# A hybrid decoder step on 8 cores: another order of work in the first two input projections

## The reference, cut to what matters

```python
h = _rmsnorm(x, norm_mix)
proj = h @ w_in                       # (B,T,2048) -> u | gb | gc | v, 512 channels each
d = trailing means of u over 2/4/8/16 positions, minus u   # 4 groups of 128 channels
a = einsum('btgc,gcd->btgd', d, w_pool) * pool_scale
conv = dwconv3_causal(gc * v)         # 3 taps
b = gb * conv
x = x + concat(a, b) @ w_out
h = _rmsnorm(x, norm_ffn)
up = dwconv3_causal(h @ w_up) + bias  # 5632 channels
x = x + (silu(gate) * val) @ w_down
y = _rmsnorm(x, norm_final)
```

## Time and profile before

| | |
|---|---|
| median of 3 runs | 730.68 us (727.58 to 747.07) |
| the profiled execution: time | 728.0 us |
| its span on the slowest core, core 3 | 726.4 us |
| spans of cores 0, 2, 4, 6 | 720.5, 720.9, 720.6, 720.1 us |
| spans of cores 1, 3, 5, 7 | 725.9, 726.4, 724.7, 724.5 us |
| PE busy | 689.3 us, 95% |
| stage 3 of tile 0 begins on core 3 at | 125.5 us |

### The profile page before, as it was taken

How to read it: one execution, slowest core, us unless ns; L and a number is a source line. 1 busy time by engine, 2 the same in 40 slices (tenths; PEclk the granted TensorE clock), 3 DMA queues, 4 the chain that set the end, 5 groups by cost and what they waited for, 6 DMA issues and landing times.

```text
span 726.4 us, 12730 instructions; the slowest of 8 cores (720.1 to 726.4 us)
## 1 busy us (share of the span) xinstructions
PE 689.3 (95%) x3788; PEld 334.7 (46%) x3788; DVE 492.2 (68%) x846; ACT 347.0 (48%) x809; POOL 215.5 (30%) x414
## 2 busy tenths in 40 slices
PE   5869799889999999999999999999999999999996
PEld 4534345445554454444444444444444444444442
DVE  4277767578886245788878566877777276888724
ACT  4344342567775112877643233766621234666521
POOL 2242100467774000455431000444420001443300
PEclk8989899989999999999999999999999999999999
DMA  8998593887787456999989430999987212980002
GB/s 198 234 170 125 97 214 62 131 146 132 126 137 152 67 164 166 172 189 187 184 150 164 145 117 1 177 166 163 155 144 123 105 71 54 162 135 1 4 29 88
DMA packets 26742, 94.62 MB, mean 130 GB/s; under 512 B 3358, under 2 KB 3742, under 8 KB 26674
## 3 DMA queue, kind: packets, MB, share of 16 engines
q0 software_dynamic: 18288, 66.59, 56.5%
q1 hardware_dynamic: 8242, 26.95, 11.1%
q10 hardware_dynamic: 144, 0.26, 0.1%
HBM read 150.36 MB, written 10.01 MB: 221 GB/s over the span
## 4 chain that ended last, share of the span: by engine, by line
PE 82%; DMA 7%; DVE 5%; issue 2%; ACT 2%; DVEq 0%; SPq 0%; ACTq 0%; POOL 0%; POOLq 0%
PE G L598 53%; PE G L905 12%; PE G L906 12%; DMA wslot<-w_str 3%; DMA yp<-x1b 3%; PE TR L598 2%; PE TR L554 2%; PE G L1142 1%; DMA x1b<-xp 1%; DVE w_down_sb L769 1%; DVE arena L769 1%; ACT hbuf L496 0%; DVE arena L830 0%; DVE arena L842 0%; DVE actT L558 0%
## 5 line engine op out<-in xcount | busy, mean ns | idle before, releaser
L969 ACT ACTIVATE arena<-G,cst_sb 128x512 f32<-128x512 f32 x176 | 135.4, 776 | 86.2 <-PE G L598 85.1
L598 PE MATMUL G<-aT,wslot 128*128 128x512 bf16 x736 | 165.8, 383 | 1.3 <-DVE arena L1007 1.0
L998 DVE SCALAR_TENSOR_TENSOR arena<-G,cst_sb,arena 128x512 f32<-128x512 f32 x176 | 124.0, 747 | 43.7 <-ACT Esave L974 41.0
L598 PE MATMUL G<-aT,sm_arena 128*128 128x512 bf16 x672 | 146.8, 379 | 0.0
L1007 DVE SCALAR_TENSOR_TENSOR arena<-G,cst_sb,arena 128x512 f32<-128x512 f32 x176 | 125.5, 744 | 4.9 <-DVE OFp L1005 0.5
L905 PE MATMUL G<-w_down_sb,actT 128*128 128x512 bf16 x330 | 125.1, 379 | 0.0
L906 PE MATMUL G<-w_down_sb,actT 128*128 128x512 bf16 x330 | 125.1, 379 | 0.0
L978 POOL TENSOR_TENSOR actT<-arena 128x512 bf16<-128x512 f32 x88 | 95.5, 1086 | 72.9 <-ACT arena L976 60.9
L598 PEld LDWEIGHTS G<-aT,wslot 128*128 128x128 bf16 x736 | 71.3, 99 | 85.3 <-issue 4.9
L598 PEld LDWEIGHTS G<-aT,sm_arena 128*128 128x128 bf16 x672 | 65.7, 98 | 78.6
L496 ACT ACTIVATE hbuf<-x1b 128x1024 bf16<-128x1024 f32 x29 | 30.7, 1057 | 136.5 <-DVE x1b L868 110.8
(11 more groups left out here) (167 smaller groups left out, 775.2 us busy)
## 6 DMA issues: line engine op xcount, KB each, us to landing
wslot<-w_str POOLq DMA_DIRECT2D x58, 512.0 KB, 7.3
sm_arena<-w_str POOLq DMA_DIRECT2D x50, 512.0 KB, 7.4
x1b<-xp SPq DMA_DIRECT2D x13, 512.0 KB, 5.0
yp<-x1b SPq DMA_DIRECT2D x12, 512.0 KB, 3.9
w_down_sb<-w_down POOLq DMA_DIRECT2D x11, 512.0 KB, 10.3
xrot<-xp SPq DMA_DIRECT2D x10, 512.0 KB, 6.3
w_down_sb<-w_str POOLq DMA_DIRECT2D x4, 512.0 KB, 18.9
w_out_sb<-w_out POOLq DMA_DIRECT2D x4, 512.0 KB, 15.0
```

The lines of the kernel that those rows point to most:

```text
L598: ins = e.matmul(out_ap, lhsT=wslot[slot][:, k, half * 128:(half + 1) * 128], rhs=rhsT[:, k, c0:c0 + ncols], start=(k == 0), stop=(k == nk ...
L969: P.op("act", lambda e, tp=tp, g=g, c=c, h=h: e.activation(out=tp[:, h, 2:514], in_=G[g][:, :], func=AF.Identity, scale=cc(C_FW + 3 * c), ...
L998: P.op("dve", lambda e, g=g, c=c, h=h: e.scalar_tensor_tensor(out=tp[:, h, 1:513], in0=G[g][:, :], scalar=cc(C_FW + 3 * c + 1), in1=tp[:, ...
```

## The change

- The four widest sums of tile 0 (u3) are emitted at pair 0 and their mean where both stood; `main_u` returns sums and mean as two functions.
- `small_cv` and `main_cv` split: the product that frees the bank is emitted at once, the convolution taps go into a list `late`, which `run_late` empties after the flush of the same pair, or for tile 1 after the next pair's bank releases. Two operations of the small convolution (the state's copy, the first tap) go from DVE to ACT.
- The small products of pairs 2 and 3 use a bank of the six, no longer a `TR` bank (`SmallBank`).
- Tile 1's last two row blocks wait for W2 instead of W1; W4 waits for the third block instead of the fourth.
- A fourth `hbuf`; in tile 0's stage 2 ACT scales the normed rows instead of DVE.
- The four folds stand behind S7, in the order 3, 2, 1, 0, with T3 and T4 between them.
- The last two pieces of `w_down` are loaded behind W14 and W18 instead of behind stage 1.
- More `keep_busy` products ahead of W0; the small block's transposes stand ahead of pair 1's products.

The core of the diff, where `...` stands for lines left out:

```diff
-        hbuf = [sb(f"hbuf{i}", [128, D], BF16) for i in range(3)]
+        hbuf = [sb(f"hbuf{i}", [128, D], BF16) for i in range(4)]
...
-                 reads=[("W", i // 2)], writes=keys, dsem=f"D_xt1_{i}")
+                 reads=[("W", (0, 0, 2, 2)[i])], writes=keys, dsem=f"D_xt1_{i}")
...
-        RES_AFTER = {4: (0, 1), 5: (2, 3), 7: (4,)}
+        RES_AFTER = {4: (0, 1), 5: (2, 3), 7: (4,), 14: (13,), 18: (14,)}
-        LATE = list(range(9, 15))
+        LATE = [9, 10, 11, 12]
-        W_AFTER = {0: [("x1", 0)], 1: [("x1", 2)], 2: [("W", 1)], 3: [("xrot", 1)], 4: [("wdown", 6)]}
+        W_AFTER = {0: [("x1", 0)], 1: [("x1", 2)], 2: [("W", 1)], 3: [("xrot", 1)], 4: [("wdown", 5)]}
...
+            def smalls(self, slot, main=False):
+                if main:
+                    g = galloc(2)
+                    h = SmallBank(G[g], gk(g), gt(g), lambda: gdone(g))
...
-                gsm = self.smalls(slot) if small else None
+                gsm = self.smalls(slot, pi in (2, 3)) if small else None
...
+                self.run_late()
...
-                        self.hold.append((at[0], fin_u))
+                        early = s == 0 and j == 3
+                        self.hold.append((0 if early else at[0], fin_u[0]))
+                        self.hold.append((at[0], fin_u[1]))
...
-                        rest = small_cv(j, gsm, half) if small else None
-                        main_cv(s, j, g, bs)
-                        if rest is not None:
-                            rest()
+                        late_s = small_cv(j, gsm, half) if small else (lambda: None)
+                        late_m = main_cv(s, j, g, bs)
+                        self.late += [late_s, late_m]
...
                 self.flush(pi)
+                if s != 1:
+                    self.run_late()
+
+            def run_late(self):
+                while self.late:
+                    self.late.pop(0)()
...
-            return norm_transpose(x1[r], 128, [("x1", r)], hb, hk, aT, i * 128, C_G2, [("aT", k, i) for k in range(8)])
+            return norm_transpose(x1[r], 128, [("x1", r)], hb, hk, aT, i * 128, C_G2, [("aT", k, i) for k in range(8)],
+                                  act_scale=(s == 0))
...
-        keep_busy(8)
+        keep_busy(24)
...
+        keep_busy(10)
...
+        keep_busy(16)
...
+        nbs.step()
         S.cols(1, ws[1], 0, 512)
-        nbs.step()
...
         for i in range(3):
             T_pair()
-            fold(i)
...
             S_pair()
+            T.run_late()
+        fold(3)
         S.flush(8)
+        fold(2)
...
         T_pair()
-        fold(3)
+        fold(1)
+        T.run_late()
         T_pair()
+        fold(0)
         n2 = [s2_block(0, 0)]
```

More of the change, by code:

```diff
@@ L567, in v3 @@
             return ap.rearrange("p (a b) -> p a b", b=b)
-        hfree = [0, 1, 2]
-        HKI = {("hb", i): i for i in range(3)}
+        hfree = [0, 1, 2, 3]
+        HKI = {("hb", i): i for i in range(4)}
         def next_hb(keep=True):
@@ L621, in __init__ @@
                 self.banks = {}
+                self.late = []
+                self.mid = None
                 self.pi = 0
@@ L691, in stage1, with subT @@
                 st.pair(next_weights(), True)
-        def subT(i, half):
-            return TRF[i][:, half * NSM:(half + 1) * NSM]
+        def subT(h, half):
+            return h.ap[:, half * NSM:(half + 1) * NSM]
         def small_u(j, gsm, half):
@@ L775, in adds, with mean @@
                 cell[0] = cur
-            def sums():
-                adds()
+            def mean():
                 cur = cell[0]
@@ L783, in sums @@
                     reads=[ab, ("UN" + tag, b)] + S3T + bs["wd"], writes=[dk(j, i) for i in range(4)] + ["arS1_dve"])
-            return sums
+            return adds, mean
         def gc_out(g, gsm, half, bs):
@@ L791, in gc_out, with small_cv @@
                 P.op("act", lambda e: e.activation(out=GCs[:, :], in_=subT(gsm, half), func=AF.Copy),
-                     reads=[("TR", gsm)], writes=["GCs", ("TRt", gsm)])
-        def small_cv(j, g_v, h_v):
+                     reads=[gsm.key], writes=["GCs", gsm.token])
+                gsm.done()
+        def small_cv(j, gsm, h_v):
             b = j % 2
@@ L797, in small_cv @@
             t = Tcs[b]
-            v_ap = subT(g_v, h_v)
+            v_ap = subT(gsm, h_v)
+            P.op("act", lambda e: e.activation(out=x[:, 5:NQ, 0:2], in_=stc_sb[:, j, :, :], func=AF.Copy),
+                 reads=[("stc", j)], writes=[("XcvS", b)])
             P.op("dve", lambda e: e.tensor_tensor(out=x[:, :, 2:6], in0=v3(v_ap), in1=v3(GCs[:, :]), op=ALU.mult),
-                 reads=[("TR", g_v), "GCs"], writes=[("XcvN", b), ("TRt", g_v)])
+                 reads=[gsm.key, "GCs"], writes=[("XcvN", b), gsm.token])
@@ L814, in rest, with taps @@
+            P.op("pool", lambda e: e.tensor_copy(out=stc_sb[:, j, :, :], in_=x[:, 5:NQ, 4:6]),
+                 reads=[("XcvN", b), ("XcvS", b)], writes=[("stc", j)])
+            def taps():
                 P.op("dve", lambda e: e.scalar_tensor_tensor(out=t[:], in0=x[:, :, 1:5], scalar=cc(C_CW + 3 * j + 1),
                                                               in1=t[:], op0=ALU.mult, op1=ALU.add),
-                     reads=[("XcvN", b), ("XcvH", b), ("Tcs", b)], writes=[("Tcs", b)])
+                     reads=[("XcvN", b), ("XcvH", b), ("XcvS", b), ("Tcs", b)], writes=[("Tcs", b)])
@@ L819, in rest @@
                      reads=[("XcvN", b), ("Tcs", b)], writes=[("Tcs", b)])
-            return rest
+            return taps
         def main_cv(s, j, g_v, bs):
@@ L1283, in build_nc @@
         pump(2)
+        pump(3)
         load_states_s1()
@@ L1334, in build_nc @@
         S_main(2)
+        nt += [norm1_block(1, i, act_scale=True) for i in range(2, 4)]
         nt[0].step()
+        nt[2].step()
         nt[1].step()
-        nt += [norm1_block(1, i, act_scale=True) for i in range(2, 4)]
-        nt[2].step()
         nt[3].step()
@@ L1342, in build_nc @@
         nt[2].step()
-        nt[3].step()
-        S.flush(2.5)
+        S.mid = nt[3].step
+        S_pair()
         scale_wpool()
-        S_pair()
         S_pair()
```

77 lines of the change are left out of this document (43 added, 34 removed).

## The result

The changed kernel takes 721.23 us, median of 4 runs (720.57 to 723.62), the kernel before 728.83 beside it (727.58 to 730.68): a ratio of 0.9899, 95% interval 0.986 to 0.9938. It is faster by 1.0%, and 721.23 lies just above the range of 706 to 721. The sum took 14.5 us off; the median fell by 7.6. All medians and ratios here leave out executions in which one die ran at a lower granted clock than the other.

A forecast was written before the change was run, and what follows sets the result against it. PE was taken to bound the kernel. Core 3: 726.4 less 9.2 from the head and 6.3 in stage 3 gives 710.9; other odd cores reach up to 712, and with 1.6 outside the span 713.5; range 706 to 721.

The forecast's parts named there:

- the price of the moved loads of w_down: Stage 3: two w_down loads placed among its weights fit into spare bandwidth; counted 0, at most 2 us.
- a wait for weights behind W14: Stage 3, sign against the forecast: new waits for weights behind W14 or W18 would prove it wrong.
- S4, T0, S5, T1, S6, T2 follow each other: Head, from S4 to S7: no waits between, 22.6 us, so S7 comes at 67.2 instead of 80.74.
- nothing gained early: Head, rival: W4 to W7 land 6 us later, S6 and S7 wait, 3 us of gain remain; 719.7, chance 0.06.
- the sum puts all cores within 1.4 us: Whole kernel: core 3 at 710.9, even cores at 710.6, cores 1, 5 and 7 up to 712.
- two neighbours that take bandwidth from each other: Paired cores sharing one HBM would compete in a tighter head; tied to the late-W12 rival, 719.8, chance 0.09.
- Pair 2 of S: Head: pair 2 starts at 29.0 instead of 31.12, if W2 is there; otherwise 1.75 us are lost again.
- The clock: First 32 products: added keep-busy products may hold the higher clock, saving 0 to 2.1 us; half, 1.05, taken.
- T3's second half: Head, before stage 2: waits for 21.5 us of DVE work and starts at 77.8.
- Stage 2 behind fold 0's ACT copies: Start of stage 2: waits 1.5 us for ACT's two copies and a handoff, beginning at 85.4 instead of 95.67.
- Two of four blocks waiting for ACT's scaling: Stage 2: PE waits 0.75 us at each of two blocks; 29.87 becomes 30.9, stage 3 begins at 116.3.
- The wait for W12 gone: Stage 3, core 3: with two w_down loads fewer ahead, W12 lands 6.5 us earlier; 6.3 us saved.

The follow-up runs named there:

- e1: Changed kernel with the two late w_down pieces moved from behind W14 and W18 to behind W22 and W26; 722.93 us, ratio 0.9915.
- e6: Changed kernel with w_out loaded behind W7 and the two late w_down pieces as eight quarter loads behind W13, W15 to W27; 717.45 us, ratio 0.9847.
- e10: Changed kernel with both late w_down pieces loaded behind W14; 726.45 us, one execution.
- e4: Changed kernel with w_out loaded behind W7 and the two late w_down pieces behind W22 and W26; 720.51 us, ratio 0.9887.
- e8: Changed kernel with w_out behind W7, late w_down pieces behind W30 and the added keep_busy products taken out; 722.79 us, ratio 0.9922.
- e11: Changed kernel with w_out behind W7, w_down pieces in quarters, tile 1's late rows and W4 ordered as before the change; 719.39 us, ratio 0.9874.
- e7: Changed kernel with w_out behind W7, late w_down pieces behind W30 and stage 2's rows scaled on DVE again; 721.73 us, ratio 0.9889.
- e9: Changed kernel with w_out behind W7, w_down pieces in quarters and stage 2's rows scaled on DVE again; 715.75 us, ratio 0.9827.
- e2: Changed kernel with the w_down split undone, so all of pieces 11 to 14 load ahead of W12 again; 724.25 us, ratio 0.9936.
- e5: Changed kernel with w_out loaded behind W7 and the two late w_down pieces behind W30; 722.0 us, ratio 0.9906.

## Why the prediction was wrong

**The step that failed** is the price of the moved loads of w_down: "0.9 us a step are free; 3.3 us of load fit into four steps. I count 0, at most 2." The share of busy DMA engines that it went by was right, and it was the wrong measure. A weight is used 7.35 us after its issue; with no piece near it W15 lands after 5.2 to 6.2, behind one piece after 7.2 to 11.2. What is left over per step doesn't help the one weight that is issued behind the piece. From the start of stage 3 to the end core 4 takes 722.1 - 121.5 = 600.6, where the forecast had 595.7 - 0.7 = 595.0 for an even core: 5.6 us more. The 595.7 is 720.6 - 124.91, where stage 3 begins on core 4 before; core 0, shown in the earlier trace rows, gives 720.5 - 124.56 = 595.9. On core 3 it is 597.8 against 594.6, 3.2. Over the eight cores it is 596.1 to 600.6, and the mean, 597.4, is that of the kernel before (595.7 to 600.9): the split exchanged the wait for W12 for waits at W15 and W19, and the gain of the profiled execution is the head's. That a wait for weights behind W14 would prove the forecast wrong was said, and that is what came; e1, e6 and e10 show the cause. The Trainium skill, DMA: Bandwidth & Descriptors, Issuing engines are not separate DMA queues, says that transfers interleave. All loads here come from POOL's queue and land in the order of their issue (on core 4 W14 at 148.5, the piece at 152.0, W15 at 156.7), so no run here tells interleaving from standing in line. The 2 us that the prediction put on that rule were too few, for the same reason as above.

**The second step** is "S4, T0, S5, T1, S6, T2 follow each other", where only W7 was asked for. W5 stood behind two loads of w_out and W6 behind four, whose reader the change itself had moved to 72.7. On core 3 S7 comes at 68.59 instead of 67.2, with 3.2 us of waits in it: the head up to S4 was better than forecast (42.51 for 43.9, at the full clock), which hid part of it. On core 4 the waits are 4.4 and half clock at S5, and stage 3 begins at 121.49. The rival "nothing gained early" thus came true in part, at S5 and S6 and by the order of the loads, not by a hole that SP's held loads leave. The sum for core 4: 124.91 - 9.2 = 115.7 forecast against 121.49, 5.8 us; with the 5.6 above that is nearly all of 722.1 - 710.6. In the mean over the cores the head falls short by 2.6 (125.55 before, 118.97 now).

**The third step** is that the sum puts all cores within 1.4 us, 710.6 to 712. The slowest core lies 5.7 us above the mean of the eight in the profiled execution and 2.5 to 3.2 in the three others, and which core it is changes. That holds for the kernel before too: in the 21 executions of it that ran beside the experiments the slowest core is an odd one in 16 and an even one in 5, and the odd core of a pair is the slower in 49 of 84 pairs. The even and odd groups that the prediction went by were those of one execution. What stays is the pair: in those executions neighbours (0 and 1, 2 and 3) differ by 3.6 us in the mean, and cores next to each other from two pairs (1 and 2, 3 and 4) by 2.5. In all 28 pairs of the kernel before, the change, e1 to e4 and e10, the core that begins stage 3 later also waits longer for weights there (core 4 of the change 4.09, core 5 1.46). That fits two neighbours that take bandwidth from each other, a rival that the prediction raised. No run has the pieces on one core of a pair only, so how much of a late weight is the neighbour's is not shown.

**What was right.** Pair 2 of S at 28.46 (29.0), with W2 0.53 late. The clock: 2.0 of the 2.1 was saved on core 3, half was taken; on 72 of the 88 cores counted under e8 more than half was saved, so half was too little. The late rows of tile 1 behind W2: e11 shows the wait for W2 that this avoids; the 1.9 us of time are not settled. T3's second half at 78.63 (77.8), waiting for DVE, as the count of DVE's work had it. Stage 2 behind fold 0's ACT copies, 1.80 (1.5). Two of four blocks waiting for ACT's scaling, 0.76 each (0.75), and e7 and e9 show that this part of the change makes stage 3 begin later. The wait for W12 gone; e2 says that without the split it would now stand on every core. The clock did not stay down between S7 and stage 2: it was 1.00 on core 3 from 60 to 118 us. Three figures of the prediction do not add up as they stand: two blocks at 0.75 make 31.4 of 29.87 and not 30.9 (measured from 86.63 to 118.33: 31.7); 5.89 and core 0's own 0.70 make 6.6 and not 6.3; half of 0.58 and 0.10 make 0.39 and not 0.45. None of them decides.

With the first two steps mended and the ACT scaling taken back, e9 stands at 715.75, 2 us above the forecast; fold 2 waits some 3.1 us for DVE there, which is the largest wait left in the head.

## What to carry to other kernels

Before a load is put into a stream that is fetched just in time, compare the time from issue to use with the time from issue to landing, not the share of busy engines: here 2 us of margin stood against 3.4 us for one load in the mean and 5.8 on the core hit hardest, and four quarters of it went in nearly free where the whole did not. When a reader is moved later, its load keeps its old place in the queue and delays what is now needed first; move it too. Where the slowest core sets the time, forecast the slow core of a pair and not one core by its number: in the profiled execution 8 to 12 us on five cores were worth little while the other three gained 3 or nothing, and the next execution has other slow cores.

## What was not expected of the hardware

One extra load makes several behind it late: in the changed kernel, core 4, W14 to W18 took 7.2, 11.2, 9.7, 8.2 and 7.8 us around one piece, and 5.4 is back only with W23, five weights behind the second piece. The same 32 first products of the same program ran at 2.8 us on five cores and at 4.3 to 4.5 on three (e5), so one core tells little of the clock at the start. Neighbouring cores move against each other in time, and which of the two is the slow one changes from execution to execution. And where a wait ends with a DMA, the trace named another engine in several cases (151.93 above, 221.89 in e5): the issue and the landing in the DMA view help there.
